# Memory keys with the weights held still and the tokens moving

## What is computed

```
mem_n = rmsnorm(mem, g_mem_kv)                 # 256 x 2048
kv = mem_n @ w_mem_kv                          # 2048 x 4096: keys, then values
k, v = kv[:, 0], kv[:, 1]                      # 4 heads of 512 each
s = einsum('bqhd,bkhd->bhqk', q, k) * 512**-0.5
o = softmax(s) @ v
x = x + rmsnorm(o @ w_mem_o, g_mem_post)
```

## Time and profile before

| | |
|---|---|
| median of 3 runs | 1797.07 us (1796.44 to 1797.71) |
| the profiled execution's own time | 1795.94 us |
| its span, first to last instruction | 1794.2 us |
| busy: PE, DVE, ACT, POOL | 99%, 64%, 53%, 3% |
| mean granted clock of PE | 0.999 of 2.4 GHz |

### The profile page before, as it was taken

The page is one execution under the profiler, slowest core; times in us unless marked ns, Lnnn a source line. Parts: engine busy times, 40 slices in busy tenths (PEclk is TensorE's granted clock), DMA queues, the critical chain, the costliest instruction groups (busy, mean ns, idle before and its releaser), DMA issues.

```text
span 1794.2 us, 25047 instructions
## 1 busy us (share of the span) xinstructions
PE 1780.8 (99%) x8758; PEld 1491.4 (83%) x8758; DVE 1155.4 (64%) x1608; ACT 951.6 (53%) x1295; POOL 59.4 (3%) x128
## 2 busy tenths in 40 slices
PE   9999999999999999999999999999999999999998
PEld 7888888888888888888888878888888888888786
DVE  5554555555465554454555477777777777788887
ACT  7555556665545655544555474444444444455554
POOL 4000000000000110000000100000000000000002
PEclk9999999999999999999999999999999999999999
DMA  8455544455466555555444546555555555656565
GB/s 287 153 188 176 166 162 148 156 170 168 167 222 221 201 189 176 183 173 190 154 146 158 189 166 232 187 187 187 187 187 187 187 187 187 199 167 206 190 197 189
DMA packets 167021, 330.74 MB, mean 184 GB/s; under 512 B 8454, under 2 KB 14006, under 8 KB 165558
## 3 DMA queue, kind: packets, MB, share of 16 engines
q1 hardware_dynamic: 165414, 318.48, 53.3%
q10 hardware_dynamic: 1552, 11.54, 1.6%
HBM read 325.81 MB, written 4.19 MB: 184 GB/s over the span
## 4 chain that ended last, share of the span: by engine, by line
PE 97%; DVE 1%; ACT 1%; DMA 0%; issue 0%; DVEq 0%; ACTq 0%
PE bank L566 17%; PE bank L979 17%; PE bank L568 17%; PE bank L567 17%; PE bank L981 9%; PE bank L1027 4%; PE bank L1028 4%; PE bank L1029 4%; PE bank L598 1%; PE bank L764 1%; PE bank L765 1%; PE bank L781 0%; PE bank L772 0%; DVE wlo L1605 0%; DVE actA L1926 0%; DMA bufX<-in_x 0%
## 5 line engine op out<-in xcount | busy, mean ns | idle before, releaser
L1605 DVE TENSOR_TENSOR wlo<-raw,whi 128x1024 fp32r<-128x1024 f32 x520 | 641.7, 1236 | 556.0 <-ACT whi L1138 433.0
L1138 ACT ACTIVATE whi<-raw 128x1024 fp32r<-128x1024 f32 x400 | 424.0, 1060 | 502.7 <-PE bank L568 293.0
L979 PE MATMUL bank<-actA,whi 128*128 128x512 f32 x1344 | 472.0, 394 | 0.0
L981 PE MATMUL bank<-actA,wlo 128*128 128x256 f32 x1344 | 380.1, 283 | 0.0
L979 PEld LDWEIGHTS bank<-actA,whi 128*128 128x128 f32 x1344 | 252.4, 188 | 58.3
L566 PE MATMUL bank<-whi,actA 128*128 128x512 f32 x672 | 273.2, 406 | 1.6 <-DVE wlo L1605 0.6
L568 PE MATMUL bank<-whi,actA 128*128 128x512 f32 x672 | 265.3, 395 | 0.0
L567 PE MATMUL bank<-wlo,actA 128*128 128x512 f32 x672 | 265.0, 394 | 0.0
L981 PEld LDWEIGHTS bank<-actA,wlo 128*128 128x128 f32 x1344 | 252.7, 188 | 0.0
L566 PE MATMUL bank<-whi,actB 128*128 128x512 f32 x576 | 229.2, 398 | 0.3 <-DVE actB L1620 0.3
L568 PE MATMUL bank<-whi,actB 128*128 128x512 f32 x576 | 227.3, 395 | 0.0
(11 more groups left out here) (278 smaller groups left out, 1869.5 us busy)
## 6 DMA issues: line engine op xcount, KB each, us to landing
raw<-in_w_ffn_in SPq DMA_DIRECT2D x88, 1024.0 KB
raw<-in_w_in SPq DMA_DIRECT2D x48, 1024.0 KB
raw<-in_w_ffn_out SPq DMA_DIRECT2D x84, 512.0 KB, 4.9
raw<-in_w_mem_kv SPq DMA_DIRECT2D x32, 1024.0 KB
raw<-in_w_attn_br SPq DMA_DIRECT2D x16, 1024.0 KB
raw<-in_w_mix_out SPq DMA_DIRECT2D x16, 1024.0 KB
raw<-in_w_mem_q SPq DMA_DIRECT2D x16, 1024.0 KB
raw<-in_w_mem_o SPq DMA_DIRECT2D x16, 1024.0 KB
```

What stands on the lines that cost most here:

```text
L979: pe.matmul(dst[:, :], whi[:, s, o:o + P], actA[:, :, kt, :], start=(kt == 0), stop=False)
L981: mm = pe.matmul(dst[:, 0:S], wlo[:, s, o:o + P], actA[:, 0, kt, :], start=False, stop=(kt == KD - 1))
L1138: act.activation(whi[:, ks % AHEAD, 0:w], raw[:, c, ks % 2, 0:w], ACT.Copy).then_inc(hi_done, 1)
L1605: dve.tensor_tensor(wlo[:, vs % AHEAD, 0:w], raw[:, c, vs % 2, 0:w], f32(whi[:, vs % AHEAD, 0:w]), ALU.subtract).then_inc(lo_done, 1)
```

## The change

Four things change.

1. **The memory's norm goes into its tokens.** In the mixer's second output column DVE multiplies memv in place, a 128x512 piece at a time, two pieces (both halves of the tokens) in each of the units k = 0 to 3; a new semaphore mem_ok counts them. PE's turning starts at k = 2 instead of 0, and the last four fills go two at a time at k = 6 and 7. The splits on ACT and DVE move with them.
2. **The keys come out turned.** `keys_column` has the form of `turned`, in the order of its output banks: the two of the first pair for all of the unit, then the two of the second. Columns alternate between the banks 2, 3, 6, 7 and 0, 1, 4, 5.
3. **No turning of keys.** `mk_job` and the evictions into kch are gone. At k = 7 ACT copies the banks' first halves into memk, ahead of its split of the next weights, and DVE adds the second halves behind its own split.
4. **Values** lose the scale in their eviction. They keep their form and count anew.

PE gets two new waits: ahead of the second key column for all the squares of x2 (`sq_done`), and ahead of the first value column for the first sum of the last key column (`keys_sum`). The loops over the key columns are written out on PE, ACT and DVE.

```diff
@@ block.tensor
         def mem_job(k):
-            if k == 0:
-                pe.wait_ge(mem_in, 16)
-            t_fill(T_MEM + k, k, memv, 2 * k)
+            for f in ((), (), (0,), (1,), (2,), (3,), (4, 5), (6, 7))[k]:
+                pe.wait_ge(mem_ok, 2 * (f // 2) + 2)
+                t_fill(T_MEM + f, f, memv, 2 * f)
...
-        def mk_job(n):
...
+        def keys_column(n):
+
+            first = FIRST[1 - n % 2]
+            for k in range(8):
+                v = V_MKV + 8 * n + k
+                pe.wait_ge(lo_done, v + 1)
+                if n == 1 and k == 0:
                     for t in range(TT):
...
+                        pe.wait_ge(acc_out[t], U_MKV)
+                    pe.wait_ge(sq_done, SQ[N_X2] + 8)
+                if n > 1 and k == 0:
+                    pe.wait_ge(keys_sum, 2 * n - 2)
+                s = v % AHEAD
+                for b in range(2):
+                    for kk in range(2):
                         for j in range(2):
...
+                            o = kk * NC + (2 * b + j) * P
+                            kt = 2 * k + kk
+                            to = bank[first[b] + j]
+                            pe.matmul(to[:, :], whi[:, s, o:o + P], actB[:, :, kt, :], start=(kt == 0), stop=False)
+                            mm = pe.matmul(to[:, 0:S], wlo[:, s, o:o + P], actB[:, 0, kt, :],
+                                           start=False, stop=(kt == KD - 1))
+                    if b == 0 and k == 7:
+                        mm.then_inc(keys_filled, 1)
+                mm.then_inc(w_used, 1)
...
+        for n in range(ND):
+            keys_column(n)
...
+        pe.wait_ge(keys_sum, 2 * ND - 1)
+        column(V_MKV + 8 * ND, U_MKV, lhsB, x2_job)
@@ block.scalar
+        def keys_column(n, job):
+
+            first = FIRST[1 - n % 2]
+            for k in range(8):
+                if k == 7:
                     for b in range(2):
...
+                        if b == 0:
+                            act.wait_ge(keys_filled, n + 1)
+                        else:
+                            act.wait_ge(w_used, V_MKV + 8 * n + 8)
+                        act.activation(memk[:, 4 * n + 2 * b:4 * n + 2 * b + 2, :],
+                                       psum[:, first[b]:first[b] + 2, 0:S], ACT.Copy).then_inc(keys_copied, 1)
+                hi_at(V_MKV, n, 8, k)
+                job(k)
+
+        for n in range(ND):
+            keys_column(n, x2_squares if n == 0 else nothing)
@@ block.vector
         def mem_split(k):
             if k == 0:
                 norm(N_MEM, 8)
-            t_split(T_MEM + k, k, *tiles(actB, 2 * k), G_MEMKV + 2 * k)
+                dve.wait_ge(rstd_done, normed(N_MEM))
+                dve.wait_ge(mem_in, 16)
+            if k < 4:
+                for t in range(TT):
+                    o = memv[:, t, k * NC:(k + 1) * NC]
+                    dve.tensor_scalar(o, o, rstd[:, N_MEM, t:t + 1], None, ALU.mult).then_inc(mem_ok, 1)
+            for f in ((), (), (0,), (1,), (2,), (3,), (4, 5), (6, 7))[k]:
+                t_split(T_MEM + f, f, *tiles(actB, 2 * f), G_MEMKV + 2 * f)
...
+        def keys_column(n, job):
+
+            first = FIRST[1 - n % 2]
+            for k in range(8):
+                lo_at(V_MKV, n, 8, k)
+                if k == 7:
+                    for b in range(2):
+                        dve.wait_ge(keys_copied, 2 * n + b + 1)
+                        keys = memk[:, 4 * n + 2 * b:4 * n + 2 * b + 2, :]
+                        dve.tensor_tensor(keys, keys, psum[:, first[b]:first[b] + 2, S:2 * S],
+                                          ALU.add).then_inc(keys_sum, 1)
+                job(k)
+
+        for n in range(ND):
+            keys_column(n, x2_job if n == 0 else nothing)
```

More of the change, by code:

```diff
@@ L107, in hybrid_layer @@
     U_MKV = U_MIX + ND
-    U_MQ = U_MKV + 2 * ND
+    U_MQ = U_MKV + ND
     U_MO = U_MQ + ND
@@ L123, in hybrid_layer @@
     A_MK = A_PAIR + 5 * NH // 2
-    A_MQ = A_MK + 2 * ND
+    A_MQ = A_MK
     N_X, N_Q, N_C, N_MEM, N_Y1, N_X2, N_Y2, N_X3, N_Y3 = range(9)
@@ L296, in hybrid_layer @@
     mrg_mul, mrg_ok = sem("mrg_mul"), sem("mrg_ok")
+    mem_ok, keys_filled, keys_copied, keys_sum = (sem(n) for n in (
+        "mem_ok", "keys_filled", "keys_copied", "keys_sum"))
     mem_in, x_again, gpost_in = sem("mem_in"), sem("x_again"), sem("gpost_in")
@@ L834, in _ @@
             column(V_MIX + 8 * n, U_MIX + n, lhsA, nothing)
-        def mk_job(n):
-            def job(k):
-                if k == 1:
-                    for t in range(TT):
-                        pe.wait_ge(acc_out[t], U_MKV + n + 1)
-                    for b in range(2):
-                        at_wait(A_MK + 2 * n + b)
-                        for j in range(2):
[L845 to L849, removed]
+        def keys_column(n):
[4 more added lines that the diff above has]
+                if n == 1 and k == 0:
+                    for t in range(TT):
+                        pe.wait_ge(acc_out[t], U_MKV)
[5 more added lines that the diff above has]
+                    for kk in range(2):
+                        for j in range(2):
+                            o = kk * NC + (2 * b + j) * P
[7 more added lines that the diff above has]
+                mm.then_inc(w_used, 1)
         pe.wait_ge(t_out, T_MEM + 8)
-        column(V_MKV, U_MKV, lhsB, nothing)
-        with pe.Fori(1, ND) as n:
-            column(V_MKV + 8 * n, U_MKV + n, lhsB, mk_job(n - 1))
+        for n in range(ND):
+            keys_column(n)
         def x2_job(k):
@@ L858, in x2_job @@
             t_fill(T_X2 + k, k, bufX, 2 * k)
[L859 to L863, removed]
+        pe.wait_ge(keys_sum, 2 * ND - 1)
+        column(V_MKV + 8 * ND, U_MKV, lhsB, x2_job)
+        with pe.Fori(1, ND) as n:
+            column(V_MKV + 8 * ND + 8 * n, U_MKV + n, lhsB, nothing)
         def mem_head(n):
@@ L1362, in mem_split @@
                 root(N_MEM)
-            t_split(T_MEM + k, k, [actB[:, 0, 2 * k + j, :] for j in range(2)], G_MEMKV + 2 * k)
+            for f in ((), (), (0,), (1,), (2,), (3,), (4, 5), (6, 7))[k]:
+                t_split(T_MEM + f, f, [actB[:, 0, 2 * f + j, :] for j in range(2)], G_MEMKV + 2 * f)
             if k == 7:
@@ L1393, in x2_split @@
             t_split(T_X2 + k, k, [actA[:, 0, 2 * k + j, :] for j in range(2)], G_MEM + 2 * k)
[L1394 to L1398, removed]
+        V_VAL = V_MKV + 8 * ND
+        column(V_VAL, U_MKV, 0, chunk(memv, 0), None, x2_split)
+        with act.Fori(1, ND) as n:
+            column(V_VAL, U_MKV, n, chunk(memv, n), None, nothing)
         def mem_head(n):
@@ L1426, in first_keys @@
             if k == 7:
+                act.wait_ge(keys_sum, 2 * ND)
                 act.activation(mk_hi, memk[:, 0:4, :], ACT.Copy).then_inc(kv_hi, 1)
@@ L1841, in x2_job @@
             residual(N_Y1, k, bufY, bufX, bufX, 0)
-        column(V_MKV, 0, x2_job)
-        with dve.Fori(1, ND) as n:
-            column(V_MKV, n, nothing)
+        def keys_column(n, job):
[11 more added lines that the diff above has]
+            keys_column(n, x2_job if n == 0 else nothing)
         def x2_split(k):
```

## The result

| | before | after |
|---|---|---|
| median | 1796.91 us (4 runs) | 1807.99 us (4 runs, 1806.9 to 1808.67) |
| span of the profiled execution | 1794.2 us | 1806.0 us |
| mean granted clock | 0.999 | 0.995 |

The ratio is 1.0061, with a 95% interval of 1.0050 to 1.0073: 11.1 us slower, against +8.0 us forecast. The median of 1807.99 us lies at the very end of the forecast range, which went to 1808.0.

The account below looks back on a forecast made before the run. The prediction took PE, busy 99% of the span, as the bound. Its terms, -3.5 + 0.7 + 5.8 + 3.8 + 1.2 = +8.0 us on the profiled 1795.94, plus 1.1 for the median, gave 1805.1 us; range 1801.5 to 1808.0.

Parts of the forecast that it names:

- The chain: Queued ACT and DVE work from a key column's last matmul: 5.8 us before the second key column, 3.8 before the values.
- The turning gone: Key columns: 32 pipelined transposes fewer on PE, 0.88 us a column, 3.5 us saved over four.
- the unit 0.02 us longer: Key product: a unit of 256 weight rows takes 2.81 us instead of 2.79, 0.7 us more over 32 units.
- the forecast rival for that case: Key and value columns: DVE's order leaves no wait, PE keeps -3.5 + 0.7 and ends at 1794.3 us; chance 0.04.
- the clock's term: Behind the wait before the second key column: PE's clock falls to half speed for a short time, costing 1.2 us.
- I let it fall in the first wait only: PE's clock falls in the 5.8 us wait before the second key column, not in the 3.8 us one before the values.
- the 4.7 us that the clock held: Program's end: the clock read full for 4.7 us behind the last matmul, then fell to 1.2 GHz.
- near the lower end: Price of the clock's fall, between nothing and 3.8 us: taken as 1.2 us, since the stall follows dense work.
- The other end of the scale: Program's start: transposes at half speed for about 7.5 us, a loss of up to 3.8 us.
- The rival with a long fall, or one in both waits: Behind the waits: clock at half as long as at the program's start, or falling twice; 1807.7 us, chance 0.10.
- The last fills: Memory's tokens: the last two fills come together at k = 7, at no cost; a few tenths if cover fails.

Follow-up runs that it names:

- Without waits: The changed kernel with x2's squares in kch instead of bank 4 and the last key column's first addition ahead of DVE's low half: 1794.17 us, ratio 0.9987.
- residual first: The changed kernel with DVE doing the last residual of x2 ahead of its two additions in the first key column: 1806.97 us.
- sum early: The changed kernel with DVE adding the first pair of banks ahead of its low half of k = 7 in the last key column: 1802.31 us.
- squares elsewhere: The changed kernel with the squares of x2 in kch instead of bank 4, and no PE wait for them before the second key column: 1799.19 us.

## Why the prediction was right, and where it was off

**Right: that it is slower, and through which waits.** Both waits are where they were put and have the releasers that were named. The chain gave 5.8 and 3.8 us. Measured from where the next matmul would have started to the restart: 5.8 us (677.88, the last 256-column matmul, to 683.75, less its step of 0.12) and 3.7 (752.91 to 756.68, less 0.12). Taking two additions out of the chain took 1.2 us out of the wait, and taking either reason away removed its wait, the second but for 0.3 us.

**Right: PE's own account.** The turning gone (-3.5), the unit 0.02 us longer (+0.7). Without waits the kernel is 2.6 us faster by the medians, and the forecast rival for that case said 1794.3 us, against 1794.17. So close a match is partly luck: the rest of the wait (0.5) and the fills (0.2) are not in its -2.8, and with them it is -2.1, which is what the stretch of the two profiles shows. The unit is 2.81 us: ACT's splits in the second key column are 2.81 apart, as in the earlier trace rows.

```profile
691.49 1.06 ACT L1137 ACTIVATE whi<-raw 128x1024 fp32r<-128x1024 f32 x1 [1.74 <-PE bank L859]
694.30 1.06 ACT L1137 ACTIVATE whi<-raw 128x1024 fp32r<-128x1024 f32 x1 [1.75 <-PE bank L859]
```

**Off: the clock's term, 1.2 us for what measured 4.6.** The step that failed is "I let it fall in the first wait only". It rested on one sample, the 4.7 us that the clock held after the program's last matmul, read as a threshold. The time from PE's last work to the fall varies: in the changed kernel it was 2.7 us in the first wait (678.16 to 680.88, worked out from 0.72 for 680 to 682) and 2.8 in the second (753.19 to 755.96, from 0.99 for 754 to 756), with residual first 3.7 and 4.0, with sum early and squares elsewhere 4.3. A wait of 3.7 us is thus enough.

The second error is the price: "near the lower end" for a stall behind dense work. The low stretch lasted on for 4.0 and 6.1 us behind the restarts, and each microsecond of it costs a little under half. The other end of the scale, half speed for 7.5 us at the start, was one sample too: in the changed kernel's own profile the second dozen of transposes there ran at full speed (1.47 us from 6.57, against 2.24 from 7.35 before).

The rival with a long fall, or one in both waits, had 1807.7 and a chance of 0.10; the fall in both waits was what came, and it should have been the likeliest. The range held the result by luck: it ended at 1808.0 only because that rival stood at its edge, and two of the four runs (1808.05 and 1808.67) lie outside.

**Off by little.** The last fills cost PE 0.2 us. By the terms: -3.5 + 0.7 + 5.8 + 3.7 + 4.6 + 0.2 = 11.5, between the 11.1 of the medians and the 11.8 of the two spans. A further 0.3 us of the spans stands in the value columns, below. The stretch from the first turning of kch to the turning of the queries holds 11.7 of the 11.8 (377.9 us against 366.2).

## What to carry to other kernels

When a kernel is bound by PE, a rearrangement that saves PE's work must first be read for the waits that it creates at the hand-over of a bank: here a gain of 2.6 us by the medians (2.1 in the profiled stretch) was covered by 14 us of waits and half speed, both removable by a change of order or of buffer. A wait of PE as long as these, 3.5 us and more, costs its own length and, behind it, a little under half of what is left of the low stretch, here 1.6 to 2.8 us; if it can't be removed, useless matmuls or transposes in it gave that second part back here. Price a transpose by how far it moves the next matmul, not by its duration.

## What the runs showed of the hardware that I had not expected

- The clock can fall behind the restart: in the squares-elsewhere run three matmuls ran at full speed after a wait of 3.5 us, and the fall came then. With residual first it came about 0.5 us behind the restart of the values.
- The low stretch, from fall to rise, lasted 6.8 us in the four falls that came inside a wait and 3.4 us in the two that came behind the restart, by the granted clock of the windows. So behind a shorter wait more of the low stretch can be left.
- Transposes alone kept the clock at 2.4 GHz over 5.2 us, in a stretch with matmuls on both sides.
- In the three profiles in which the clock fell at the start of the value columns, the memory's values from the first to the last eviction took 69.1 or 69.2 us; in all others, the kernel before among them, 68.8 or 68.9, with the same matmuls. The rows of the changed kernel and of the one without waits:

```profile
L1163 ACT ACTIVATE memv<-bank x8: 597/598/598, 783.8 to 852.9; 128x512 f32 x6, 128x512 f32<-128x512 f32 x2
```
```profile
L1163 ACT ACTIVATE memv<-bank x8: 597/598/601, 770.3 to 839.1; 128x512 f32 x6, 128x512 f32<-128x512 f32 x2
```

The units there are 2.80 us in place of 2.79, at a granted clock of 1.00. Why a stretch that ended at 763 us leaves the matmuls 0.4% slower for 80 us was not tried.
